# Right products of the inverse's first level and both products of its second on 32x32 quarters of the array instead of 64x64 halves, in the RWKV-7 stage of a two-layer hybrid step

## What is computed

```python
def rwkv_scan(r, w, k, v, kk, a, s0):
    def step(s, inp):
        r_t, w_t, k_t, v_t, kk_t, a_t = inp
        sa = jnp.einsum('bhvk,bhk->bhv', s, -kk_t)
        s = s * w_t[:, :, None, :] + sa[..., None] * (kk_t * a_t)[:, :, None, :] + v_t[..., None] * k_t[:, :, None, :]
        return s, jnp.einsum('bhvk,bhk->bhv', s, r_t)
    ...
    s_fin, out = lax.scan(step, s0.astype(f32), xs)
```

## Time and profile before

| What | us |
|---|---|
| median of 3 runs | 1650.57 (1645.33 to 1650.81) |
| time of the profiled execution | 1650.08 |
| its span, first to last instruction | 1648.3 |
| TensorE busy (share of the span) | 1459.5 (89%) |
| VectorE, ScalarE, GpSimd busy | 603.4, 526.3, 264.7 |
| mean granted TensorE clock | 0.951 of full speed |

### The profile page before, as it was taken

One profiled execution on the slowest core, in us unless ns is written; L12 is line 12 of the kernel. 1 busy time (PEld: TensorE's weight loads), 2 busy tenths in 40 slices (PEclk: granted clock), 3 DMA queues, 4 the chain that ended last, 5 costly groups with the idle time before them and its releaser, 6 DMA issues. The chain is left out here.

```text
span 1648.3 us, 41176 instructions
## 1 busy us (share of the span) xinstructions
PE 1459.5 (89%) x17678; PEld 925.1 (56%) x17678; DVE 603.4 (37%) x1520; ACT 526.3 (32%) x1202; POOL 264.7 (16%) x260
## 2 busy tenths in 40 slices
PE   3998878887999999859998888888879779999997
PEld 1555457445555555535555777777755555555554
DVE  2002674234111111461123777777751521111116
ACT  2113463222112112130134666666541311211112
POOL 0000023002000000110014556666510100000010
PEclk8899799899899999979999999999999989999999
DMA  9323645837699999902210000000004469999992
GB/s 388 132 101 131 258 175 235 345 119 306 236 381 369 378 376 370 395 26 102 102 51 3 6 6 6 6 6 6 6 4 179 157 270 362 372 372 376 379 386 90
DMA packets 54037, 328.34 MB, mean 199 GB/s; under 512 B 6646, under 2 KB 10038, under 8 KB 18712
## 3 DMA queue, kind: packets, MB, share of 16 engines
q1 hardware_dynamic: 43632, 290.07, 45.8%
q0 software_dynamic: 5184, 18.88, 2.9%
q10 hardware_dynamic: 5096, 17.58, 2.7%
HBM read 304.35 MB, written 22.16 MB: 198 GB/s over the span
## 5 line engine op out<-in xcount | busy, mean ns | idle before, releaser
L1398 PE MATMUL ps<-ring,arena 128*64 128x256 f32 x2048 | 244.3, 387 | 6.0 <-ACT arena L1513 4.9
L1398 PEld LDWEIGHTS ps<-ring,arena 128*64 128x64 f32 x2048 | 142.5, 138 | 97.2 <-issue 36.6
L298 PE MATMUL ps<-HT,ring 128*128 128x384 f32 x544 | 180.8, 496 | 14.2 <-PEq L367 8.2
L298 PEld LDWEIGHTS ps<-HT,ring 128*128 128x128 f32 x544 | 105.5, 195 | 89.4 <-issue 20.1
L1408 PE MATMUL ps<-ring,arena 128*32 128x128 f32 x4096 | 133.3, 277 | 0.0
L1602 DVE TENSOR_TENSOR arena<-arena,ps 64x256 f32<-64x256 f32 (+1 forms) x128 | 40.6, 358 | 253.3 <-ACT arena L1519 253.3
L1434 PE MATMUL ps<-ring,arena 128*64 128x512 f32 x512 | 129.9, 605 | 0.0
L1518 ACT ACTIVATE arena<-ps 64x256 f32<-64x256 f32 x64 | 24.1, 377 | 310.3 <-PE ps L1398 310.3
L1408 PEld LDWEIGHTS ps<-ring,arena 128*32 128x32 f32 x4096 | 107.4, 111 | 26.9 <-issue 25.4
L298 PE MATMUL ps<-arena,ring 128*128 128x384 f32 x256 | 85.2, 497 | 18.8 <-DVEq L2053 18.8
L1526 ACT ACTIVATE arena<-ps 32x256 f32<-32x256 f32 x128 | 47.8, 374 | 160.4 <-PE ps L1434 159.2
(11 more groups left out here) (358 smaller groups left out, 2237.0 us busy)
## 6 DMA issues: line engine op xcount, KB each, us to landing
ring<-wstream SPq DMA_DIRECT2D x272, 1024.0 KB, 7.4
moe_rows<-arena ACTq DMA_DIRECT2D x28, 384.0 KB, 7.1
arena<-moe_tokens POOLq DMA_DIRECT2D x12, 512.0 KB, 16.2
moe_rows<-arena ACTq DMA_DIRECT2D x4, 512.0 KB
consts<-cst ACTq DMA_DIRECT2D x1, 1655.0 KB, 17.1
XT<-xT ACTq DMA_DIRECT2D x1, 1536.0 KB, 11.1
yT<-HT SPq DMA_DIRECT2D x3, 384.0 KB, 3.2
arena<-wa SPq DMA_DIRECT2D x1, 1024.0 KB, 4.8
```

The lines of the kernel that those rows point to most:

```text
L298: mm = pe.matmul(bank(m % 8), w[:, k, m % 2 * P:m % 2 * P + P], rhs[:, k, :], start=k == 0, stop=k == KC - 1)
L1398: mm = pe.matmul(bank(h, 256)[HD * x:HD * x + HD], TOKE[:, k, 0:MANY], w[:, kk, x, :], start=k == 0, stop=k == KC - 1)
```

## The change

Three of the eight products of levels 1 to 4 get another form: right at level 1, left at level 2, right at level 2, each for both directions. At these levels all blocks lie within 32x32 diagonal blocks, so a product of 64x64 by 64x32 splits into two of 32x32 by 32x32. The new function makes, for each chunk, four products, one for each quarter of the partitions, on the four diagonal 32x32 parts of the array, with 32 columns and no broadcast copy. On VectorE the mask's multiplication at level 2 reads the 32 columns twice through a broadcast instead of reading 64, and the subtraction reads 32 adjacent columns instead of the first 32 of each 64. Shapes and counts on VectorE stay.

```diff
+        LEFT_QUARTERS, RIGHT_QUARTERS = (2,), (1, 2)
...
             def left_dve(dve, c, n, d):
                 dve.wait_ge(s_ll, c * NLL + (2 * n - 1 + d))
+                p_ = bank(LEFT_BANKS[d], NCH * 32).rearrange("p (n j) -> p n j", j=32)
                 if n == NLEV:
-                    p_ = bank(LEFT_BANKS[d], NCH * 32).rearrange("p (n j) -> p n j", j=32)
                     dve.tensor_copy(dn(PF)[:, d, :, 0:32], p_).then_inc(s_ls, 1)
                     return
                 mask = msk1(C_LEV + 2 * (n - 1) * CH, d)
-                dve.tensor_tensor(dn(PF)[:, d].rearrange("p n (b j) -> p n b j", b=2),
-                                  bank(LEFT_BANKS[d], NCH * HD).rearrange("p (n b j) -> p n b j", b=2, j=32),
+                both = bank(LEFT_BANKS[d], NCH * HD).rearrange("p (n b j) -> p n b j", b=2, j=32)
+                if n in LEFT_QUARTERS:
+                    both = p_.unsqueeze(2).broadcast_to([P, NCH, 2, 32])
+                dve.tensor_tensor(dn(PF)[:, d].rearrange("p n (b j) -> p n b j", b=2), both,
                                   mask.rearrange("p n (b j) -> p n b j", b=2), ALU.mult).then_inc(s_ls, 1)
...
                 once = bank(RIGHT_BANKS[d], NCH * HD).rearrange("p (n b j) -> p n b j", b=2, j=32)[:, :, 0]
+                if n in RIGHT_QUARTERS:
+                    once = bank(RIGHT_BANKS[d], NCH * 32).rearrange("p (n j) -> p n j", j=32)
...
+            def quarters_pe(pe, o, left, right, d):
+                for n in range(NCH):
+                    for q in range(4):
+                        rows, at = slice(32 * q, 32 * q + 32), 32 * (q % 2)
+                        mm = pe.matmul(bank(o, 32, 32 * n)[rows], dn(left)[rows, d, n, at:at + 32], right[rows, d, n],
+                                       start=True, stop=True)
+                return mm
...
             def left_pe(pe, c, n, d):
                 pe.wait_ge(s_inv, c * NINV + (2 * n - 1 + d))
-                if n < NLEV:
+                if n in LEFT_QUARTERS:
+                    mm = quarters_pe(pe, LEFT_BANKS[d], AF, DC, d)
+                elif n < NLEV:
                     mm = each(pe, LEFT_BANKS[d], AF, DC, d)
...
             def right_pe(pe, c, n, d):
                 pe.wait_ge(s_ls, c * NLL + (2 * n - 1 + d))
-                if n < NLEV:
+                if n in RIGHT_QUARTERS:
+                    mm = quarters_pe(pe, RIGHT_BANKS[d], PF, DTC, d)
+                elif n < NLEV:
                     mm = each(pe, RIGHT_BANKS[d], PF, DTC, d)
```

## The result

The changed kernel takes **1653.76 us** (median of 20 runs, 1649.61 to 1659.99), the kernel before in the same comparison 1648.30 (20 runs). The ratio is 1.0034 with a 95% interval of 1.0025 to 1.0044: 0.34% slower, 4.1 to 7.3 us on 1648.3, and within the half per cent that was called "the same". The profiled execution of the changed kernel is the longest of its runs, 1659.99 us; part of its excess is granted clock outside the stretches compared here (0.94 behind the recurrence, against 0.96 in the kernel before), so pairs are compared only where the clock was full.

The account below looks back on a forecast made before the run. Bound: a chain of waits across engines, through the second `lora_pe` to left (4,0). 6 x 0.58 - 0.1 + 0.58 = +4.0 on 1650.08 gives 1654.1; the median, 0.5 above, gives 1654.5 us, range 1645.5 to 1662.5.

Parts of the forecast that it names:

- A change of form drains TensorE: On TensorE, a product of another shape starts only 0.07 us before the last ends, so quarters and crossed products lose overlap.
- The case of no drain: Rival: quarters slip between crossed records on TensorE, `lora_pe` comes 0.41 us earlier, -3.8 in all, 1646.8 us; chance 0.12.
- The quarter product: On TensorE, a quarter product of 48 records takes 0.57 us instead of 0.92, letting the next start after 0.50.
- Right (1,0) ahead of it: Level 1, ahead of the crossed products: right (1,0) ends 0.35 us earlier, of which VectorE's first subtraction gains 0.09.
- Crossed to `lora_pe`: TensorE, middle pair: first crossed product to second `lora_pe` grows from 3.25 to 3.92 us, 0.67 more; 0.58 later after 0.09 gained.
- Left (4,0), and through it the pair, hangs on: Second `lora_pe` starts ScalarE's chain, which releases left (4,0) on TensorE; that sets the pair, 0.58 us later.
- The wait for L2194: Sign of being right: TensorE's idle ahead of left (4,0) is still put down to that ScalarE line, formerly L2193.
- The ends: First and last pair of the recurrence: first about -0.1 us, last +0.58 us through left (3,0).
- The sum: Whole kernel: 6 x 0.58 for middle pairs, -0.1 for the first, +0.58 for the last, +4.0 us.
- The bound by issue at 16 ns a record: Rival: 48 records on TensorE take 0.76 us to issue, a quarter product ends after 0.95; +11, 1661.5 us; chance 0.14.
- The floor of 25 ns from start to start: Rival: TensorE records start at least 25 ns apart, 48 need 1.2 us; +22 in all, 1672 us; chance 0.04.
- The clock: Rival: the emptier array lowers the granted clock in each pair, about +1.0 x 8 on the forecast, 1662 us; chance 0.05.

Follow-up runs that it names:

- e3: Kernel before with only the right product of level 1 on quarters, order unchanged; ratio to before 1.0003.
- e7: Changed kernel with quarters at left and right of level 4 instead, halves elsewhere; ratio to the kernel before 1.0055.
- e5: Changed kernel with left (2,1) moved ahead of the wait and both crossed products on TensorE; ratio to the kernel before 1.0041.
- e4: Changed kernel with quarters at left and right of levels 3 and 4 instead, halves at 1 and 2; ratio to the kernel before 1.0117.
- e14: As e13, with the right product of level 2 on quarters too; ratio to the kernel before 1.0014.
- e11: Changed kernel with only left at level 2 on quarters, second `lora_pe` right after left (2,1), crossed products after right (2,1); 1643.72 us, ratio to before 0.9971.
- e13: As e11, with VectorE's second scan moved next to the first; ratio to the kernel before 0.9980.
- e12: TensorE order of e11 with all products of levels 1 to 4 on halves, so only order differs from the kernel before; ratio 0.9998.
- e8: As e5, but only the left product of level 2 on quarters; ratio to the kernel before 0.9990.
- e10: As e5, but with the right product of level 1 back on halves; ratio to the kernel before 0.9990.

## Why the prediction was right, and where it was off

The forecast of 1654.5 stands 0.7 above what was measured, in the case called the likeliest. Part of that closeness is luck: the change was put at +4.0 and measured at +5.5, and the median of three runs that it was added to, 1650.57, stands 2.3 above the 1648.30 of the comparison. By its steps:

- **A change of form drains TensorE.** Right. Left (2,1) starts 0.07 before the last crossed record's end, as in the earlier trace rows, and crossed alone is 1.53 long with the next start after 1.46, to the hundredth. The case of no drain fell: no quarter record lies between crossed ones. The Trainium skill (TensorEngine Tiling (Array Packing), section "Key Properties") says that a change of tiling mode drains TensorE. These rows agree, and put the larger price not on the drain but on the overlap that one form had with itself, since right (1), between products of other forms before as after, lost nothing.
- **The quarter product.** Mis-sized. I took 0.57 from level 5; it is 0.62, and the next start comes after 0.55, not 0.50. Four parts take 12 turns of 0.43 / 12 = 36 ns, where two took 32. Twice 0.05 makes 0.10 of the 0.19 by which a pair was off.
- **Right (1,0) ahead of it.** The step that failed: "0.09 gained on 938.27" never came. I took VectorE's 0.14 behind the memset for a wait for TensorE; with right (1,0) done earlier it is 0.15, and e3 changes the pair by 0.01. The program has VectorE wait there for its own memset to end, which fits; no run tested it. That is the other 0.09.
- **Crossed to `lora_pe`.** Forecast +0.67, measured +0.76; for the pair +0.58 and +0.77.
- **"Left (4,0), and through it the pair, hangs on" `lora_pe`.** The start was right, the way only half so. Left (4,0) still waits for the same ScalarE line, but e7 shows that what is saved there alone is given back: GpSimd's chain from the same sigmoids is longer by less than 0.1 us. I had left GpSimd out because it is busy for 25.3 of 42.2 us, and did not see that these 25 us are one chain with both ends tied. The size held because both chains begin at `lora_pe`, which I did not know: that was luck. The wait for L2194, which I had named as a sign of being right, shows what left (4,0) waits for and not what the pair hangs on.
- **The ends.** First pair: 43.36 instead of 43.49, -0.13 for a forecast of -0.1. Last pair, first crossed record to left (3,0): 1204.81 - 1199.86 = 4.95 instead of 1199.17 - 1194.98 = 4.19, +0.76 for +0.58, the same mis-sizing.
- **The sum.** With the measured terms 6 x 0.77 - 0.13 + 0.76 = 5.25, for a measured 4.1 to 7.3; forecast 4.0.
- **The rivals.** The bound by issue at 16 ns a record fell for a product by itself: 96 records in a row start over 1.04 - 0.19 = 0.85, 9 ns apart, and none ended after 0.95. The floor of 25 ns from start to start that the Trainium skill gives (TensorE: Matmul & The Clock Gate, section "Wait — 56ns, not 53.3ns?") does not hold for parts in different rows of the array here. A bound by the supply of instructions came at a larger scale, in e5, e7, e4 and e14. The clock stayed as before in the changed kernel: 0.99 over the recurrence (884 to 1232 us), against 0.98.

## What to carry to other kernels

A cheaper form of a product pays only if the products around it on TensorE have that form too, or if nothing there overlapped; group products by form before splitting some. Follow a late event through every engine that it releases, also one that looks half idle: its 25 us may be a single chain, and then whatever is saved behind the fork is given back where the chains meet. A wait that stands ahead of a product does not show that the time hangs on it; an experiment that shortens only what follows it does. Of all edits tried, those that paid most (e11 and e13) moved the product at the fork to an earlier place and had the cheaper form where it lost no overlap. The early place with halves (e12) gained nothing, the cheaper form without overlap lost but `lora_pe` in its old place (e8) 0.1%.

## What was not expected of the hardware

- TensorE idles for issue, 0.2 to 1.6 us at a time, where many small products follow closely: not once in the kernel before, 0.4 us once with the change, 4.9 in e5, 12.1 in e4, and gone in e10 with 12 products fewer per direction. The limit is the supply of instructions: each such idle ends 1.20 to 1.59 us after a packet of 16 KB has landed on the queue that brings them. The count of packets alone does not decide: it is 96 before, 105 in e5 but also in the changed kernel, and 102 in e7 as in e10, which has no such idle. In the recurrence two packets never start less than 3.3 us apart in any of the fourteen kernels; whether that is the rate at which the supply gives out was not measured by itself.
- The granted clock falls to half now and then in every one of these kernels, in the one before from 1141.8 to 1145.2 without any idle for issue. About some of those idles it stays there longer, in e7 from 1126.5 to 1140 about the one of 1.38, and a usual pair of e7 with both was 44.59 to 46.67 us long, 2.4 to 4.5 more than one with neither. That the idle brings the low clock is not shown: in e5 one of 0.89 ends at 1114.45, and the clock is full up to 1140.
- VectorE and GpSimd block each other on instructions that read two operands from SBUF, in both directions: a sum of 0.32 became 1.02 (e7), a scan of 0.94 became 2.53 and a multiplication of 1.81 became 2.47 (e11).
